# Down projection of an encoder layer: the loads of the seventh and eighth left operand move ahead in the load queue, the second gate and the first x1 tiles behind them

## The reference

```python
h2 = rmsnorm(x, g_ffn) * (1 + scale2) + shift2
ff = (jax.nn.silu(h2 @ w_gate) * (h2 @ w_up)) @ w_down
return x + gate2 * ff
```

## Time and profile before

| | |
|---|---|
| time, 3 runs | median 1671.11 us (1669.94 to 1673.9) |
| the profiled execution | 1670.68 us, span 1668.9 us, mean granted clock 0.994 |
| PE busy | 1625.4 us (97% of the span), 7939 matmuls |
| DVE, ACT, POOL busy | 1052.8 us (63%), 644.2 us (39%), 173.9 us (10%) |
| chain that ended last | PE 62% of the span, DMA 2%, SP's queue 2%, DVE 1% |

### The profile page before, as it was taken

How to read it: one execution, slowest core, us unless ns; L and a number is a source line. 1 busy time by engine, 2 the same in 40 slices (tenths; PEclk the granted TensorE clock), 3 DMA queues, 4 the chain that set the end, 5 groups by cost and what they waited for, 6 DMA issues and landing times.

```text
span 1668.9 us, 20970 instructions
## 1 busy us (share of the span) xinstructions
PE 1625.4 (97%) x7939; PEld 1300.2 (78%) x7939; DVE 1052.8 (63%) x1679; ACT 644.2 (39%) x1121; POOL 173.9 (10%) x123
## 2 busy tenths in 40 slices
PE   5999999999999999999999999999999998999998
PEld 3767888866676888888888888888888886888887
DVE  3524888058968453444564698888777764668774
ACT  4512333158765243433332333433333333343330
POOL 0311222000000232100000000000000001314060
PEclk9999999999999999999999999999999999999999
DMA  9771010433220432444454233433333476767773
GB/s 349 285 239 49 26 38 26 88 61 32 59 89 26 164 139 101 149 136 120 134 144 145 73 120 107 120 102 109 106 95 95 157 259 248 248 226 266 249 249 99
DMA packets 222072, 230.63 MB, mean 138 GB/s; under 512 B 25272, under 2 KB 169874, under 8 KB 221850
## 3 DMA queue, kind: packets, MB, share of 16 engines
q1 hardware_dynamic: 221017, 226.21, 43.2%
q0 software_dynamic: 960, 3.15, 0.5%
HBM read 183.30 MB, written 46.02 MB: 137 GB/s over the span
## 4 chain that ended last, share of the span: by engine, by line
PE 62%; DMA 2%; SPq 2%; DVE 1%; ACT 0%; issue 0%; DVEq 0%; ACTq 0%
PE banks L99 20%; PE banks L101 20%; PE banks L100 20%; PE banks L2429 1%; SPq L1767 1%; DMA a_raw<-fc_rows 1%; DMA fc_rows<-s_join 1%; SPq L1748 0%; DVE s_sum L2180 0%; DMA s_raw<-in_w_up 0%; DMA s_raw<-in_w_gate 0%; DVE s_lo L2190 0%; DMA fc_rows<-s_up 0%; SPq L1735 0%; DVE a_lo L2234 0%
## 5 line engine op out<-in xcount | busy, mean ns | idle before, releaser
L99 PE MATMUL banks<-b_hi,a_hi 128*128 128x512 f32 x462 | 181.1, 392 | 7.1 <-DVE a_lo L2234 4.5
L100 PE MATMUL banks<-b_lo,a_hi 128*128 128x512 f32 x462 | 180.7, 391 | 0.0
L101 PE MATMUL banks<-b_hi,a_lo 128*128 128x512 f32 x462 | 180.6, 391 | 0.0
L99 PE MATMUL banks<-h_hi,p_hi 128*128 128x512 f32 x352 | 138.5, 394 | 0.0
L101 PE MATMUL banks<-h_hi,p_lo 128*128 128x512 f32 x352 | 137.2, 390 | 0.0
L100 PE MATMUL banks<-h_lo,p_hi 128*128 128x512 f32 x352 | 137.0, 389 | 0.0
L99 PE MATMUL banks<-h_hi,s_hi 128*128 128x512 f32 x352 | 136.9, 389 | 0.0
L100 PE MATMUL banks<-h_lo,s_hi 128*128 128x512 f32 x352 | 136.9, 389 | 0.0
L101 PE MATMUL banks<-h_hi,s_lo 128*128 128x512 f32 x352 | 136.9, 389 | 0.0
L99 PE MATMUL banks<-h_hi,win_hi 128*128 128x512 f32 x336 | 132.4, 394 | 3.6 <-DVE h_lo L523 2.8
L100 PE MATMUL banks<-h_lo,win_hi 128*128 128x512 f32 x336 | 131.4, 391 | 0.0
(11 more groups left out here) (263 smaller groups left out, 3405.5 us busy)
## 6 DMA issues: line engine op xcount, KB each, us to landing
a_raw<-fc_rows SPq DMA_DIRECT2D x40, 704.0 KB, 4.8
b_raw<-in_w_down SPq DMA_DIRECT2D x77, 256.0 KB, 5.4
ada_rest<-in_w_ada SPq DMA_DIRECT2D x16, 1024.0 KB, 8.5
b_second<-in_w_down SPq DMA_DIRECT2D x55, 256.0 KB, 5.9
p_raw<-in_w_gate SPq DMA_DIRECT2D x22, 512.0 KB, 3.8
p_raw<-in_w_up SPq DMA_DIRECT2D x22, 512.0 KB, 3.9
s_raw<-in_w_gate SPq DMA_DIRECT2D x11, 1024.0 KB, 5.4
s_raw<-in_w_up SPq DMA_DIRECT2D x11, 1024.0 KB, 5.3
```

The lines of the kernel that those rows point to most:

```text
L99: pe.matmul(out, lhs[0], rhs[0], start=start, stop=False)
L100: pe.matmul(out, lhs[0], rhs[1], start=False, stop=False)
L101: return pe.matmul(out, lhs[1], rhs[0], start=False, stop=stop)
```

## The change

SP's transfers are the same 481 in both programs; five places in the queue move. `load_a(6)` goes up, directly behind `load_a(5)`, and waits only for its buffer; the two loads of b for j = 6 no longer wait for `s_stored`; `load_a(7)` goes up ahead of the second gate and the x1 tiles, which keep their wait.

```diff
             sp.wait_ge(used, D0 + 2)
             load_a(5)
-            sp.wait_ge(s_stored, 112 * JN - 16)
+            sp.wait_ge(used, D0 + 3)
+            load_a(6)
             sp.wait_ge(b_ready, B0 + JN)
             for quad in second:
-                if quad[0] >= 6:
+                if quad[0] == 6:
                     load_b(1, quad)
+            sp.wait_ge(s_stored, 112 * JN - 16)
+            for quad in second:
+                if quad[0] > 6:
+                    load_b(1, quad)
+            sp.wait_ge(used, D0 + 4)
+            load_a(7)
             sp.dma_start(gate2[:].rearrange("p r n -> p (r n)"), bass.AP(gate_rows.tensor, 2 * D, [[0, 128], [1, 2 * D]])
                          ).then_inc(gate2_in, 16)
             sp.wait_ge(x1_stored, 16 * NCH)
             for g in range(4):
                 load_part(g)
-            for n in range(2, DN):
+            for n in range(4, DN):
```

## The result

| | before | after |
|---|---|---|
| time, 4 runs each | median 1672.51 us (1669.94 to 1674.65) | median 1663.95 us (1661.57 to 1665.75) |
| ratio | | 0.9944, 95% interval 0.9929 to 0.9960 |
| the profiled execution | 1670.68 us, span 1668.9 | 1665.75 us, span 1664.0 |
| from the first load of a(2), which waits for the end of the stage before, to the end of the span | 1668.9 - 1339.79 = 329.1 us | 1664.0 - 1343.99 = 320.0 us |

What follows compares the result with a forecast made beforehand. PE was taken to lose 9.97 us by j = 7 of unit 6, waiting on ACT and DVE. Earlier a(6) 9.65 less 0.65 for j = 6 gives 9.0: 1670.68 to 1661.7, plus 0.43, 1662.1 us; range 1660 to 1665.5.

Steps and rivals of the forecast that it cites:

- a(6): On ACT: issued directly behind a(5), it is rounded from about 1376.44 without a wait for it, 9.65 us earlier.
- The pair of j = 6: On DVE: the sums for j = 0 wait for these b loads and start 0.65 us later (bounds 0 and 2.1).
- PE's remaining wait: On PE ahead of j = 7 in unit 6: one wait of 1.0 us for a low part of b.
- a(7): On ACT: it lands at 1382.0 and is rounded at 1384.2, so 2.2 us remain and ACT hides it.
- second rival: On ACT: a(7), behind a(6) and ten b loads, becomes the wait; gain 5.7 us, 1665.4 us; chance 0.08.
- first rival: In SP's queue: a(5) shares the engines with a(6) and lands 1.74 us later; gain 7.9, 1663.2 us; chance 0.12.
- Unit 8 and the stores: Two rivals: PE waits for a(8), 1671.1 us, chance 0.05; `s_stored` comes 18 us late, 1675 us, chance 0.03.
- The clock: On PE in unit 6: it stays up over the 1.0 us wait, as at the 2.63 us wait before.

Runs made afterwards that it cites:

- Experiment 2: Against the changed kernel: a(6) and the j = 6 loads put behind the wait for the stores, a(6) after all ten b loads, before the gate; ratio 0.9973.
- kernel 1: Against the changed kernel: a(7) put back behind the gate and the four x1 tiles; ratio 0.9958 to the kernel before.
- experiment 5: Against the changed kernel: the two b loads for j = 6 put back behind the wait for the stores; ratio 0.9941 to the kernel before.
- experiment 6: Against the changed kernel: a(5) ahead of the last six stores, j = 6 loads with j = 4 and 5, a(7) ahead of j = 9 and 10; ratio 0.9935.
- first repeat of kernel 1: kernel 1 profiled again with nothing changed; down projection 323.6 us, PE lost 4.6 us.
- before again: The kernel before, unchanged, profiled once more; down projection 330.4 us, PE lost 11.4 us.
- second repeat of kernel 1: kernel 1 profiled once more with nothing changed; down projection 324.9 us, PE lost 6.0 us.

## Why the prediction was right

The time, 1663.95, is in the range and 1.85 above the forecast; the median of the kernel before, which the forecast started from, came out 1.4 higher (1672.51, with one run more). The gain was forecast as 9.0 us and is 9.1 in the down projection of the profiles and 8.6 in the medians.

- **a(6)** is rounded without a wait, 1381.17 - 1343.99 = 37.2 us into the down projection; forecast was 1376.44 + 0.65 - 1339.79 = 37.3. Right. Experiment 2 shows that its place in the queue is the larger part of the gain.
- **The pair of j = 6** as the new wait on DVE: right in kind, and too small for this execution. The sums start 1377.68 - 1373.74 = 3.94 us after a(5)'s rounding, against 3.02 before: 0.92 later, not 0.65. In the three executions of kernel 1 they start 0.40, 0.55 and 0.65 later, so the term's size is not off beyond this scatter. The pair needs 2.2 us after a(6) here, not 1.9: a(6) is issued some 0.7 us after 1368.36 and lands after 6.3 us, `b_second` of j = 6 lands 7.6 us after its issue at 1370.06. These are the landings, of a(6):

```profile
a_raw<-fc_rows SPq DMA_DIRECT2D x2, 704.0 KB, 5.8
```

(the median of the two issued at 1368.36 and after it, 5.35 and 6.3 us) and of the pair:

```profile
b_raw<-in_w_down SPq DMA_DIRECT2D x1, 256.0 KB, 6.4
b_second<-in_w_down SPq DMA_DIRECT2D x1, 256.0 KB, 7.6
```

- **PE's remaining wait**, 1.0 forecast and 1.0 measured, is in part luck: the pair cost 0.27 more, and a(5) came 0.40 earlier in this execution (1369.94 - 1339.79 = 30.15 before, 29.75 after), while PE came to unit 6 0.15 earlier too. The executions with a(5) behind the stores have it rounded 29.2 us (experiment 2) to 30.75 us (experiment 5) after the first load of a(2), and the forecast took this as fixed.
- **a(7)**: forecast 2.2 us to spare; it landed at 1376.35 + 8.8 = 1385.2 and was rounded at 1388.27, 3.1 to spare; the eight loads ahead of it landed 0.72 us apart, not 0.84. Experiment 1 shows that it is needed: behind the gate it becomes the wait. So the second rival named a mechanism that is real, at a rate of the queue that did not come.
- **The first rival**, a(5) held up by a(6), is out: a(5) landed 5.35 us after its issue, and in experiment 2, where no `a` load stands behind it, 5.3:

```profile
a_raw<-fc_rows SPq DMA_DIRECT2D x1, 704.0 KB, 5.3
```

  By the rule of the Trainium skill (DMA: Bandwidth & Descriptors, Queues, rings and completion order) completion need not follow the order of issue. The traces agree, by small amounts: in the changed kernel `b_second` of j = 6, issued at 1370.06, landed at 1377.66 (7.6 us, above), and the first load of j = 7, issued at 1372.03, landed 0.2 us before it:

```profile
b_raw<-in_w_down SPq DMA_DIRECT2D x1, 256.0 KB, 5.4
```

  In experiment 6 `b_raw` of j = 9 landed 0.5 us before a(7) (1378.43 + 6.26 = 1384.69 against 1377.96 + 7.25 = 1385.21), which was issued just ahead of it. So "in the order of issue" holds here only to some tenths of a us. a(5) was not delayed.

- **Unit 8 and the stores**: PE has no wait at unit 8 (a(8) landed 1392.08 - 1343.99 = 48.1 us in; forecast was 1389.6 - 1339.79 = 49.8), and the wait for the stores ended 1372.03 - 1343.99 = 28.04 us in, against 28.44 before. Neither rival cost anything.
- **The clock** stayed at 1.00 after the short wait, as forecast. But I read from the earlier trace rows that a wait of 2.63 us does it no harm; in other executions waits hardly longer did (last section).

## What to carry to other kernels

When a wait of the bounding engine follows a long series on other engines, look for the first transfer that the series waits for and for what stands ahead of it in an in-order queue for no reason of its own: here 2 MB for a later stage and a wait for stores that the operand doesn't read. Count each move by what lands next and when it is wanted; issuing a load earlier gained nothing here while the queue ahead of it was full (experiment 5). And compare profiled executions by stage, from a marker in the program, since what lies ahead of the change can scatter by more than a small gain (here by up to 6 us between profiles).

## What was not expected of the hardware

TensorE's clock after a wait: it stayed at 1.00 after waits of 0.84 and 2.63 us, and fell to 0.50 (1.2 GHz) at or after waits of 2.85 (first repeat of kernel 1), 2.87 and 4.35 (before again), 3.43 (experiment 1), 3.95 (experiment 2), 4.25 (second repeat of kernel 1) and 4.46 us (before). In both repeats, and at the wait of 2.87, it fell only 0.8 to 1.5 us after the matmuls had gone on, as stretches of the first repeat show (1.5 and 2 us):

```profile
1397.00:1398.50 1.50, 1.12 (x5) 0.93 (x6) 1.50 (x4) 1.50 (x4) 0.00 (x0) 1.00 0.00 0
1399.00:1401.00 2.00, 2.00 (x6) 1.52 (x5) 1.34 (x2) 0.69 (x1) 0.00 (x0) 0.50 0.38 118
```

Where there was one fall, it cost PE 1.6 (both repeats of kernel 1) to 2.7 us (experiment 2) on top of the wait. And the pair of loads that experiment 5 issued 2.4 us later, counted from a(5)'s issue, landed 0.3 to 0.8 us sooner after a(5) than in the four executions with a(6) and the pair right behind a(5); in the changed kernel the queue got nothing more for 1.3 us behind that pair. Why the pair is slower then was not tried.
